# Four hybrid layers on one core: order, banks and buffers at the seams of the softmax layers

## The chip, the cores and the metric

The kernel runs on one core of a Trainium2 chip. What is measured is the time of one execution on the device, in microseconds (us); smaller is better.

## The reference

A sequence of 512 tokens with 1024 features passes four layers. Each layer has a mixer and a convolutional feed-forward part, each between two RMS norms with a residual:

```python
for layer in range(DEPTH):
    kind, j = layer % N_MIXERS, layer // N_MIXERS
    u = rms_norm(h, norm_g[layer, 0])
    u = nsa_mixer(...) if kind == 0 else stick_breaking_mixer(...) if kind == 1 else swa_sink_mixer(...)
    h = h + rms_norm(u, norm_g[layer, 1])
    u = conv_ffn(rms_norm(h, norm_g[layer, 2]), ...)
    h = h + rms_norm(u, norm_g[layer, 3])
```

The kinds are nsa, sb, swa, nsa. All have 16 heads of 64. The nsa mixer adds three gated attentions, over compressed, selected and window keys, with four key groups of four heads each; at this length selected and window keys see all earlier tokens, and each is a softmax over `q k^T / 8 - slope * distance` with the slope `2 ** (-(head + 1) / 2)`. The swa mixer is one softmax over the last 128 tokens with a sink term, with two key groups. The sb mixer weights values by sigmoids and a running product. The feed-forward part multiplies by 1024 x 5632, convolves over three tokens, gates with silu and multiplies by 2816 x 1024.

## The kernel before

Activations lie transposed: `h`, `xh`, `xl` are 8 chunks of 128 features by 512 tokens. Weight products are made from split numbers: a weight unit (128 x 1024) is loaded into a ring of four, ACT copies its high part (`split_hi`, L260), DVE subtracts the low part (`split_lo`, L266), and PE multiplies high by high, low by high and high by low (L304 to L306). Four units make a panel, which fills four of the eight PSUM banks; panel p takes banks 4 to 7 if p is odd. `panel_free` makes PE wait until the panel two before has been evacuated. Splits run three units ahead of PE.

Every engine has its own program, written out by hand in an order, with semaphores between them. Around a mixer it is this:

**Norm seam** (`pe_post`, `act_rn`, `dve_update`, `act_update`, `pool_h_squares`). PE sums squares, ACT makes the factor rn in two halves, DVE makes chunk 0 of the normed input (`dh`, L531, L534), and ACT copies it to `xh` (L577), for which the first products (`first_panel`, L332 to L338) wait. ACT splits a weight unit between rn and this copy. DVE then updates chunks 1, 2, 3, 0, 4 to 7 (L515, L516), each followed by the low part `xl` (L497) of the one before, and splits a unit (`split_lo`) after chunk 4. POOL adds the squares of h as soon as four are there. Chunks 0 to 3 come from a copy of the first output panel, chunks 4 to 7 from the second panel in PSUM. Only ahead of the sb layer (`stays(s)` false) the second panel is copied to `late_u` first, as the sb mixer's first panel goes to the same four banks.

**nsa mixer.** Query, compressed, gate, selected-key and window-key panels are multiplied in turn (`pe_nsa`); mixing of the compressed attention (`turned`, `mixed`, L1387 and L1395) is placed between the units of the window panel. Its third and fourth token blocks wait for the second of two `pt` buffers and for the output copies on ACT. Then `pe_attention` runs: four turns (`it`, one key group each), in which heads r, key kinds b (0 selected, 1 window) and four query tiles i follow each other. For each tile PE makes scores (L1052, L1053) four tiles ahead, DVE adds the distance table and takes the minimum (`biased`, L1121), ACT takes the exponential (L1213), PE turns the tile (L1063), ACT or DVE copies it to `pt`, PE multiplies by values (L1073), and DVE scales the output of a job (four tiles) into `om` (L1158), which POOL adds to `o` (L1267). Queries are split for each head by ACT and DVE into one of two `qs` buffers (L1205, L1104). POOL makes a table slope x distance for each head in one of two `tb` buffers (L1256). The window keys are copied (`act_k`) and their low parts made (`dve_k_low`) after the first four tiles of scores, ahead of everything else of the first turn. The score banks are 0 to 3, turned tiles and outputs are in 4 to 7.

**End.** When all jobs are added, `pe_out` turns `o` (L1291) column by column, ACT and DVE split it to `xh` and `xl`, four columns ahead of the first output product.

**swa mixer** (`pe_swa`). Queries, keys with values, and the second half of the queries are multiplied, DVE scales the queries (`dve_q`), then the same attention runs with b = 0 alone and 256 or 128 keys for a tile.

Of the kernel before, what the change touches and what calls it, by code (L numbers as in the profile page):

```python
# [6 lines left out]
F32 = mybir.dt.float32  # L7
# [12 lines left out]
H = 16  # L20
# [21 lines left out]
MIX_PANELS = {"nsa": 8, "sb": 7, "swa": 3}  # L42

MIX_READS = {"nsa": [(1, 0), (1, 0), (0, 1), (1, 0), (1, 1), (0, 0), (1, 1), (0, 0)], "sb": [(0, 0)] + [(1, 0)] * 4 + [(0, 1)] * 2,
# [59 lines left out]
def hybrid_layers(nc, ins, out, kinds=KIND):  # L104
# [7 lines left out]
    with ExitStack() as ctx:  # L112
# [53 lines left out]
        late_u = Space(40 * K, 48 * K)("late_u", [P, 4, T], F32)  # L166
# [10 lines left out]
        bank_done = sem("bank_done")  # L177
        units_done = sem("units_done")
# [113 lines left out]
        def unit_products(pe, p, u, xhi, xlo, first, last, i=None):  # L292


            pe.wait_ge(split_done, at(i, 4, u + 1))
            unit_matmuls(p, u, xhi, xlo, first, last, last)

        def unit_matmuls(p, u, xhi, xlo, first, last, by_bank):
# [4 lines left out]
            for k, o in order:  # L303
# [3 lines left out]
                if by_bank and k == 1 and o < 3:  # L307
                    mm.then_inc(bank_done, 1)
# [33 lines left out]
        def after_rsum(pe, p, u0, n, by_token):  # L342
# [9 lines left out]
            for j in range(4):  # L352
                pe.wait_ge(split_done, u0 + j + 1)
                unit_matmuls(p, u0 + j, lambda k: xh[:, 2 * j + k, :], lambda k: xl[:, 2 * j + k, :], j == 0, j == 3,
                             False) if j else first_by_bank(p, u0, sums_taken)
# [13 lines left out]
        def x_panel(pe, p, u0, n, i=None, step=0, turn=4, ready=None, output=False, before=None):  # L369

            panel_free(pe, p, i, step)
            for j in range(4):
                if before:
# [5 lines left out]
                             output and j == 3)  # L379
# [59 lines left out]
        def stays(s):  # L439


            return s % 2 == 0 or s + 1 == 2 * len(kinds) or kinds[(s + 1) // 2] != "sb"

        def dve_take_u(dve, s, p, u):
# [3 lines left out]
            dve.wait_ge(u_done, 4 * (s + 1) + 4 * sum(not stays(x) for x in range(s)))  # L448
            dve.sem_inc(evac_v, 1)

        def dve_sum_squares(dve, s, p):

            def take(o):
                if not stays(s):
                    dve.wait_ge(sq_done, 8 * s + 5 + o)
                    nc.vector.tensor_copy(late_u[:, o, :], bank(p, o)).then_inc(u_done, 1)

            dve.wait_ge(ss_done, s + 1)  # L460
            for o in range(3):
# [3 lines left out]
                if o < 2:  # L465
                    take(o)
            take(2)
            take(3)
            if not stays(s):
                dve.wait_ge(u_done, 4 * (s + 1) + 4 * sum(not stays(x) for x in range(s + 1)))  # L470
                dve.sem_inc(evac_v, 1)
# [19 lines left out]
        def dve_update(dve, ch, s, u, p, u_split, g_post, g_pre):  # L491
# [16 lines left out]
            def update(c):  # L508
                if c < 4:
                    src, d = u[:, c, :], dh[:, c % 2, :]  # L510
                elif stays(s):
                    src = d = bank(p, c - 4)
                else:
                    src, d = late_u[:, c - 4, :], dh[:, c % 2, :]
# [29 lines left out]
            low(2)  # L544
            update(0)
            for c in range(4, DC):
# [3 lines left out]
                if c == 4:  # L550
                    split_lo(dve, u_split)
            low(DC - 1)
            if stays(s):
                dve.sem_inc(evac_v, 1)

        def act_update(act, s, g_pre, first_units=False):
# [9 lines left out]
            if s < 0:  # L566
                for c in range(DC):
# [3 lines left out]
                    if first_units and c % 2:  # L571
                        split_hi(act, c // 2)
# [9 lines left out]
            for k, c in enumerate((1, 2, 3, 0, 4, 5, 6, 7)):  # L582
# [3 lines left out]
                square(k, c)  # L586

# [135 lines left out]
        def dve_ffn(dve, ch, l, n, s):  # L723
# [22 lines left out]
            dve_sum_squares(dve, s, plan.down_p[l] + 1)  # L746
# [19 lines left out]
        tb = soft("tb", [P, 2, T], F32)  # L766
# [38 lines left out]
        qs = Space(u2_at + 4 * K, u2_at + 8 * K)("qs", [P, 2, T], F32R)  # L805
        om = Space(u2_at, u2_at + 4 * K)("om", [P, 2, TC, DH], F32)
# [22 lines left out]
        v_passed = sem("v_passed")  # L829
        g_passed = sem("g_passed")  # L830
# [16 lines left out]
        k_ready = sem("k_ready")  # L847
        v_ready = sem("v_ready")
# [14 lines left out]
        tb_done = sem("tb_done")  # L863
# [14 lines left out]

        JOBS = {"nsa": 2 * H, "swa": H, "sb": 0, None: 0}
# [1246 lines left out]
```

## Time and profile before

| | us |
|---|---|
| median of 3 timed runs | 2695.88 (2695.68 to 2696.88) |
| profiled execution | 2692.94 |
| its span, first to last instruction | 2691.2 |
| PE busy | 2576.8 |
| DVE busy | 1652.7 |
| ACT busy | 1178.2 |
| POOL busy | 354.6 |

A busy time is the sum over an engine's instructions in that one execution; the chain that ended last lies on PE for 84% of the span and on DVE for 12%. In the rows, "idle <- releaser" is the time for which the engine stood still before an instruction, with what ended it.

### The profile page before, as it was taken

To read this page: it belongs to the slowest core of one execution; us is meant where nothing else is said; L and a number is where in the kernel's file an instruction comes from. 1 tells how busy PE (TensorE), PEld (TensorE's weight loads), DVE (VectorE), ACT (ScalarE), POOL (GpSimd) and SP (SyncE) were. 2 spreads that over 40 slices of the span, in tenths; PEclk is the share of its full clock that TensorE was granted. 3 is DMA by queue.
4 is the path that set the end of the run, shared out by engine and by line. 5 is a ranking of instruction groups with operands and counts; after the bars stand their busy time and mean duration, and the time that the engine had idled before them with its cause. 6 is when DMAs were issued, how large, how long until landed. Compare 5 with 4: busy or idle time off the path is not lost.

```text
span 2691.2 us, 38440 instructions
## 1 busy us (share of the span) xinstructions
PE 2576.8 (96%) x13432; PEld 2176.4 (81%) x13432; DVE 1652.7 (61%) x2869; ACT 1178.2 (44%) x1827; POOL 354.6 (13%) x298
## 2 busy tenths in 40 slices
PE   8989999999999889999999999999999899999997
PEld 6879978888878567888878878888779898788886
DVE  7567667665363857777355767764376675676733
ACT  4356544443232745444234544442333664444431
POOL 1012221110010002111010021110010121211100
PEclk9999999999999999999999999999999999999999
DMA  4400023322233012332322023323333000233321
GB/s 156 135 30 2 1 85 104 101 94 95 79 106 94 16 49 86 94 98 81 111 75 71 21 84 101 100 94 97 96 103 101 17 2 32 86 95 96 99 94 55
DMA packets 62054, 210.93 MB, mean 78 GB/s; under 512 B 8673, under 2 KB 10465, under 8 KB 61921
## 3 DMA queue, kind: packets, MB, share of 16 engines
q1 hardware_dynamic: 61920, 209.14, 24.6%
q8 instruction: 85, 1.39, 0.2%
q14 instruction: 49, 0.39, 0.0%
HBM read 207.02 MB, written 2.10 MB: 78 GB/s over the span
## 4 chain that ended last, share of the span: by engine, by line
PE 84%; DVE 12%; ACT 2%; issue 1%; DMA 0%; DVEq 0%; POOL 0%; SPq 0%; ACTq 0%; POOLq 0%
PE psum L304 20%; PE psum L305 20%; PE psum L306 20%; PE psum L1073 6%; PE psum L1063 3%; PE psum L917 2%; PE psum L918 2%; PE psum L919 2%; DVE left L1910 2%; PE psum L1053 2%; PE psum L1052 2%; PE psum L338 1%; DVE h L516 1%; DVE w_lo L266 1%; DVE xl L497 1%
## 5 line engine op out<-in xcount | busy, mean ns | idle before, releaser
L304 PE MATMUL psum<-xh,w_hi 128*128 128x512 f32 x1736 | 678.6, 391 | 4.6 <-DVEq L979 3.7
L305 PE MATMUL psum<-xh,w_lo 128*128 128x512 f32 x1736 | 677.3, 390 | 0.0
L306 PE MATMUL psum<-xl,w_hi 128*128 128x512 f32 x1736 | 676.9, 390 | 0.0
L266 DVE TENSOR_TENSOR w_lo<-w_raw,w_hi 128x1024 fp32r<-128x1024 f32 x226 | 288.7, 1291 | 520.5 <-ACT w_hi L260 518.8
L260 ACT ACTIVATE w_hi<-w_raw 128x1024 fp32r<-128x1024 f32 x226 | 235.5, 1057 | 572.9 <-PE psum L306 450.6
L304 PEld LDWEIGHTS psum<-xh,w_hi 128*128 128x128 f32 x1736 | 326.7, 188 | 73.5 <-DVEq L979 4.1
L306 PEld LDWEIGHTS psum<-xl,w_hi 128*128 128x128 f32 x1736 | 326.7, 188 | 67.6
L305 PEld LDWEIGHTS psum<-xh,w_lo 128*128 128x128 f32 x1736 | 326.7, 188 | 66.9
L720 DVE TENSOR_TENSOR w_lo<-w_raw,w_hi 128x1024 fp32r<-128x1024 f32 x160 | 209.2, 1308 | 253.6 <-ACT w_hi L716 253.6
L305 PE MATMUL psum<-ah,w_lo 128*128 (+1 forms) x704 | 274.2, 389 | 0.0
L304 PE MATMUL psum<-ah,w_hi 128*128 (+1 forms) x704 | 274.2, 389 | 0.0
L306 PE MATMUL psum<-al,w_hi 128*128 (+1 forms) x704 | 274.2, 389 | 0.0
L716 ACT ACTIVATE w_hi<-w_raw 128x1024 fp32r<-128x1024 f32 x160 | 168.4, 1052 | 234.8 <-PE psum L306 234.8
L691 POOL TENSOR_TENSOR cv<-cv 128x512 f32<-128x512 f32 x88 | 133.8, 1520 | 796.1 <-ACT cv L645 792.1
L1073 PE MATMUL psum<-v,pt 128*128 128x65 f32 x1504 | 212.1, 270 | 7.0 <-DVE pt L1169 5.4
L1073 PEld LDWEIGHTS psum<-v,pt 128*128 128x128 f32 x1504 | 204.3, 193 | 16.1 <-DVE pt L1169 9.7
L640 ACT ACTIVATE cv<-xo,conv_b,conv_w 128x512 f32<-128x512 f32 x176 | 129.2, 806 | 95.5 <-DVE xo L664 95.5
L673 DVE SCALAR_TENSOR_TENSOR cv<-xo,conv_w,cv 128x512 f32<-128x512 f32 x176 | 169.7, 1004 | 0.7 <-DVE xo L664 0.7
L1213 ACT ACTIVATE scores<-scores,mins 128x256 f32<-128x256 f32 (+1 forms) x320 | 162.0, 538 | 2.1 <-DVE mins L1121 1.5
L1121 DVE CUSTOM_DVE_ANT_0 scores<-psum,tb 128x512 f32<-128x512 f32 (+3 forms) x256 | 123.8, 485 | 57.0 <-PE psum L1053 53.7
L306 PEld LDWEIGHTS psum<-al,w_hi 128*128 128x128 f32 x704 | 132.2, 188 | 27.5
L304 PEld LDWEIGHTS psum<-ah,w_hi 128*128 128x128 f32 x704 | 132.2, 188 | 27.4
(193 smaller groups left out, 3870.9 us busy)
## 6 DMA issues: line engine op xcount, KB each, us to landing
w_raw<-w_up SPq DMA_DIRECT2D x176, 512.0 KB, 3.6
w_raw<-w_down SPq DMA_DIRECT2D x88, 512.0 KB, 3.6
w_raw<-nsa_in SPq DMA_DIRECT2D x56, 512.0 KB, 3.9
w_raw<-sb_in SPq DMA_DIRECT2D x24, 512.0 KB, 3.7
w_raw<-nsa_out SPq DMA_DIRECT2D x16, 512.0 KB, 3.6
w_raw<-swa_in SPq DMA_DIRECT2D x10, 512.0 KB, 3.7
w_raw<-sb_out SPq DMA_DIRECT2D x8, 512.0 KB, 3.6
w_raw<-swa_out SPq DMA_DIRECT2D x8, 512.0 KB, 3.7
```

Source lines behind the costliest of these rows:

```text
L260: nc.scalar.activation(w_hi[:, u % RING, :], w_raw[:, u % RING, :], ACT.Copy).then_inc(hi_done, 1)
L266: nc.vector.tensor_tensor(w_lo[:, u % RING, :], w_raw[:, u % RING, :], w_hi[:, u % RING, :].bitcast(F32), ALU.subtract).then_inc(split_don ...
L304: nc.tensor.matmul(bank(p, o), wh[:, k, o, :], xhi(k), start=(first and k == 0), stop=False)
L305: nc.tensor.matmul(bank(p, o), wl[:, k, o, :], xhi(k), start=False, stop=False)
L306: mm = nc.tensor.matmul(bank(p, o), wh[:, k, o, :], xlo(k), start=False, stop=(last and k == 1))
L640: nc.scalar.activation(cv[:, o, :], xo[:, o, 2:T + 2], ACT.Identity, bias=conv_b[:, bass.ds(cc, 1)], scale=conv_w[:, 2, bass.ds(cc, 1)]).t ...
L673: marks.append(ch.then(nc.vector.scalar_tensor_tensor(cv[:, o, :], xo[:, o, 1:T + 1], conv_w[:, 1, bass.ds(cc, 1)], cv[:, o, :], ALU.mult, ...
L691: nc.gpsimd.tensor_tensor(cv[:, 2 + a, :], cv[:, a, :], cv[:, 2 + a, :], ALU.mult).then_inc(prod_done, 1)
L716: nc.scalar.activation(w_hi[:, u % RING, :], w_raw[:, u % RING, :], ACT.Copy).then_inc(hi_done, 1)
L720: nc.vector.tensor_tensor(w_lo[:, u % RING, :], w_raw[:, u % RING, :], w_hi[:, u % RING, :].bitcast(F32), ALU.subtract).then_inc(split_don ...
L1073: mm = nc.tensor.matmul(psum[:, 6 + job % 2, i * (DH + 1):(i + 1) * (DH + 1)], pt[:, s % 2, j * P:(j + 1) * P], vt[b][:, k0 + j, it, :], s ...
L1213: nc.scalar.activation(sp_[:, s % 4, 0:nk * P], sp_[:, s % 4, 0:nk * P], ACT.Exp, scale=-1.0, bias=mins[:, c:c + 1]).then_inc(exp_done, 1)
```

## The change

- **Order of tiles.** In a turn all four heads run over the selected keys first (b = 0), then all four over the window keys. `qs` has four buffers; each head's queries are split in the turn before. The window keys' copies are cut up: POOL copies four halves ahead of its additions, ACT copies the four others (`win_twin`) and DVE makes the low parts (`win_low`) between tiles of the first turn.
- **No slope tables.** Queries are divided by the head's slope when split, and DVE's minimum multiplies by it; the distance table is the same for all heads, so POOL makes no tables and has nothing to do in the swa layer.
- **Banks.** `half_of(l, k)` is `k ^ 4`: scores are in banks 4 to 7, the rest in 0 to 3, in all mixers. The sb mixer has one panel number fewer, so its first panel goes to the other four banks; `late_u` and `stays` are gone.
- **Mixing.** The turning of blocks 2 and 3 stands in the middle of window unit 2, the mixing of 2 and 3 in the middle of unit 3; blocks 2 and 3 have `late_pt` buffers of their own. The first scores come before the wait for the evacuation of the window panel. ACT takes the last mixed outputs and the window values after two queries.
- **swa.** The first four tiles of scores stand ahead of the last unit of the second query panel, which tells of each bank (`qb_done`); DVE scales the queries bank by bank after its first four minima.
- **Turning of o.** Columns 0 to 2 are turned between the last tiles, and the first output unit starts with chunk 0 alone; its third and fourth banks wait for the last two jobs.
- **Norm seams.** ACT's weight split goes behind the first square of h, DVE's ahead of the update of chunk 0.

```diff
-MIX_PANELS = {"nsa": 8, "sb": 7, "swa": 3}
+MIX_PANELS = {"nsa": 8, "sb": 6, "swa": 3}
...
-            return [(b, r, i, win[i][0], win[i][1]) for r in range(R) for b in range(nb) for i in reversed(range(TC))]
+            return [(b, r, i, win[i][0], win[i][1]) for b in range(nb) for r in range(R) for i in reversed(range(TC))]
...
@@ dve_update
             update(3)
             low(2)
+            split_lo(dve, u_split)
             update(0)
             for c in range(4, DC):
                 dve.wait_ge(h_done, 8 * s + c)
                 update(c)
                 low(c - 1)
-                if c == 4:
-                    split_lo(dve, u_split)
@@ act_update
                 square(k, c)
+                if k == 0:
+                    split_hi(act, u_split)
@@ pe_attention, turn
                     if more or s + 4 < n:
                         scores(it, s + 4)
+                    elif kind == "nsa" and s + 1 < n:
+                        pe_turn_o(pe, l, s + 4 - n)
                     if s:
                         values(s - 1)
+                if kind == "swa":
+                    if not more:
+                        pe_turn_o(pe, l, 0)
+                        pe_turn_o(pe, l, 1)
                 values(n - 1)
+                if kind == "swa" and not more:
+                    pe_turn_o(pe, l, 2)
@@ dve_attention, biased
-                if i == TC - 1 and b == 0:
-                    dve.wait_ge(tb_done, it * R + (h0 + R * w + r + 1))
...
-                dve.sem_inc(v_passed, 1)
-                x = nc.vector.tensor_tensor_reduce(out=sp_[:, s % 4, 0:nk * P], in0=psum[:, s % 4, 0:nk * P], in1=bias,
-                                                   scale=1.0, scalar=lowest(it, w, r) if kind == "swa" else 3e38,
+                x = nc.vector.tensor_tensor_reduce(out=sp_[:, s % 4, 0:nk * P], in0=psum[:, half_of(l, s % 4), 0:nk * P], in1=away,
+                                                   scale=slope(R * (it + w) + r), scalar=lowest(it, w, r) if kind == "swa" else 3e38,
@@ dve_attention
+                    if kind == "nsa":
+                        if it == 0 and s in WIN_LOW:
+                            win_low(WIN_LOW.index(s))
+                        if more and s >= 16 and s % 4 == 3:
+                            queries(it + 1, s // 4 - R)
...
+        WIN_TWIN = (1, 6, 12, 17)
+        WIN_LOW = (2, 4, 8, 10, 14, 16, 20, 22)
@@ act_attention, ahead
                 queries(0, 0)
                 queries(0, 1)
+                if late and kind == "nsa":
+                    late()
+                    queries(0, 2)
+                    queries(0, 3)
@@ act_nsa
-            act_attention(act, l, "nsa", lambda: act_k(act, l, 1, 2, 2))
+
+            def between():
+                mixed(2)
+                mixed(3)
+                act_v(act, ch, 1, p0 + 6, u0 + 28)
+
+            act_attention(act, l, "nsa", between)
@@ pe_nsa
-            window(2)
+            window(2, turn_late)
             mixed(0)
-            turned(2)
-            turned(3)
-            window(3)
             mixed(1)
-            mixed(2)
-            mixed(3)
+            window(3, mix_late)
             pe.wait_ge(co_ready, TC * (k + 1))
-            panel_free(pe, W + 2)
...
+            def first(scores):
+                scores()
+                panel_free(pe, W + 2)
@@ pool_nsa
-            pool.wait_ge(cp_ready, 2 * (k + 1))
+            for g in range(G):
+                pool.wait_ge(kt_done, kc_before[l] + 2 + g // 2 + 1)
+                s_ = slice(64 * (g % 2), 64 * (g % 2) + 64)
+                nc.gpsimd.tensor_copy(kh[1][s_, g, :], ktmp[s_, g // 2, :]).then_inc(wkh_done, 1)
@@ pe_out
+            for k in range(2):
+                pe.wait_ge(o_ready, 8 * l + k + 1)
+                for o in range(4):
+                    if k == 0 and o >= 2:
+                        pe.wait_ge(om_done, jobs - 3 + o)
+                    mm = three(bank(p, o), wh[:, k, o, :], wl[:, k, o, :], xh[:, k, :], xl[:, k, :], k == 0, False)
+                if k == 0:
+                    pe_turn_o(pe, l, 3)
@@ pe_swa
+            def late_queries(first_scores):
+                def begin(j):
+                    if j == 3:
+                        panel_free(pe, p0 + 3)
...
+                        first_scores()
+
+                x_panel(pe, p0 + 2, u0 + 6, n, banks=qb_done, before=begin)
+                panel_free(pe, p0 + 4)
@@ dve_nsa
-            for c in range(2):
+            low_flat(0)
             dve_q(dve, ch, l, 0, p0 + 1, u0 + 8, -SCALE, qt)
+            low_flat(1)
```

## Rows read from the trace of the kernel before

**Rows 1.** Head of the page: busy time, share, instructions of each engine.
```profile
PE 2576.8 (96%) x13432; PEld 2176.4 (81%) x13432; DVE 1652.7 (61%) x2869; ACT 1178.2 (44%) x1827; POOL 354.6 (13%) x298
```

**Rows 2.** Busy time by stretches: us, engines (x instructions), granted clock, DMA share, GB/s.
```profile
143.40:181.44 38.04, 28.87 (x165) 25.36 (x165) 21.10 (x42) 18.16 (x32) 2.85 (x2) 0.87 0.13 42
...
181.40:217.30 35.90, 35.77 (x305) 34.84 (x305) 27.58 (x116) 24.65 (x53) 9.81 (x12) 1.00 0.01 1
...
1466.00:1522.00 56.00, 50.10 (x431) 47.34 (x430) 48.78 (x201) 42.85 (x117) 7.97 (x13) 1.00 0.00 1
```

**Rows 3.** Timeline of PE, first nsa attention start: start, us, operation, count, [idle<-releaser].
```profile
144.28 1.09 PE L1387 MATMUL psum<-ident,scores 128*128 128x128 f32 x8 [0.88 <-DVE scores L1614]
...
159.09 1.89 PE L1395 MATMUL psum<-cvb,pt 128*128 128x256 f32 x8
...
168.29 0.47 PE L1052 MATMUL psum<-kh,qs 128*128 128x512 f32 x1 [2.73 <-DVE qs L1104]
...
174.10 1.12 PE L1063 MATMUL psum<-ident,scores 128*128 128x128 f32 x4 [4.19 <-ACT scores L1213]
...
181.44 0.61 PE L1063 MATMUL psum<-ident,scores 128*128 128x128 f32 x4
```

**Rows 4.** Timeline of ACT in the same stretch.
```profile
159.29 1.57 ACT L995 ACTIVATE v<-psum,rt 128x256 f32<-128x256 f32 x4 [5.42 <-PE psum L919]
...
166.80 1.28 ACT L1205 ACTIVATE qs<-qt 64x512 fp32r<-64x512 f32 x2
...
168.10 5.20 ACT L953 ACTIVATE kh<-ktmp 64x512 fp32r<-64x512 f32 x8
...
173.33 1.23 ACT L1213 ACTIVATE scores<-scores,mins 128x512 f32<-128x512 f32 x2
```

**Rows 5.** DVE groups, shapes apart: shapes, count | busy us, mean ns | idle before.
```profile
L266 DVE TENSOR_TENSOR w_lo<-w_raw,w_hi 128x1024 fp32r<-128x1024 f32 x226 | 288.7, 1291 | 520.5 <-ACT w_hi L260 518.8 <-DVE qt L976 1.0 <-DVE xcf L1540 0.3
...
L1121 DVE CUSTOM_DVE_ANT_0 scores<-psum,tb 128x512 f32<-128x512 f32 x64 | 44.2, 691 | 46.2 <-PE psum L1053 46.2
...
L1104 DVE TENSOR_TENSOR qs<-qt,qs 64x512 fp32r<-64x512 f32 x48 | 32.9, 686 | 13.3 <-ACT qs L1205 11.9
```

**Rows 6.** Timeline of PE, end of the first nsa attention.
```profile
319.29 0.98 PE L1073 MATMUL psum<-v,pt 128*128 128x65 f32 x6
...
322.57 3.22 PE L1291 MATMUL psum<-ident,o 128*128 128x128 f32 x16 [2.29 <-POOL o L1267]
...
325.69 0.77 PE L304 MATMUL psum<-xh,w_hi 128*128 128x512 f32 x1
```

**Rows 7.** Timeline of PE, start of the swa attention.
```profile
1458.71 0.36 PE L1052 MATMUL psum<-kh,qs 128*128 128x256 f32 x1 [4.33 <-DVE qs L1104]
...
1460.50 0.69 PE L1063 MATMUL psum<-ident,scores 128*128 128x128 f32 x2 [0.66 <-ACT scores L1213]
...
1466.07 0.60 PE L1063 MATMUL psum<-ident,scores 128*128 128x128 f32 x2
```

**Rows 8.** Timeline of PE, end of the swa attention.
```profile
1525.88 0.47 PE L304 MATMUL psum<-xh,w_hi 128*128 128x512 f32 x1 [0.96 <-DVE xl L1302]
```

**Rows 9.** Timelines of ACT, DVE and PE in the norm seam after the first nsa.
```profile
374.48 0.42 DVE L534 TENSOR_TENSOR dh<-dh 128x256 f32<-128x256 f32 x1
...
374.63 1.04 ACT L260 ACTIVATE w_hi<-w_raw 128x1024 fp32r<-128x1024 f32 x1
...
375.58 0.71 ACT L577 ACTIVATE xh<-dh 128x256 fp32r<-128x256 f32 x2
...
386.14 2.31 DVE L266 TENSOR_TENSOR w_lo<-w_raw,w_hi 128x1024 fp32r<-128x1024 f32 x1
...
391.65 1.20 PE L338 MATMUL psum<-xl,w_hi 128*128 128x512 f32 x4 [0.82 <-DVE xl L497]
```

**Rows 10.** Timeline of PE in the norm seam before the sb layer.
```profile
755.89 1.20 PE L338 MATMUL psum<-xl,w_hi 128*128 128x512 f32 x4 [1.38 <-DVE xl L497]
...
761.20 1.21 PE L338 MATMUL psum<-xl,w_hi 128*128 128x512 f32 x4 [2.30 <-DVE xl L497]
```

More of the change, by code:

```diff
@@ L367, in first_by_bank, with x_panel @@
             mm.then_inc(units_done, 1)
-        def x_panel(pe, p, u0, n, i=None, step=0, turn=4, ready=None, output=False, before=None):
+        def x_panel(pe, p, u0, n, i=None, step=0, turn=4, ready=None, banks=None, before=None):
             panel_free(pe, p, i, step)
@@ L447, in dve_take_u, with dve_sum_squares @@
                 nc.vector.tensor_copy(u[:, o, :], bank(p, o)).then_inc(u_done, 1)
-            dve.wait_ge(u_done, 4 * (s + 1) + 4 * sum(not stays(x) for x in range(s)))
+            dve.wait_ge(u_done, 4 * (s + 1))
             dve.sem_inc(evac_v, 1)
[L451 to L458, printed above, removed]
+        def dve_sum_squares(dve, s):
             dve.wait_ge(ss_done, s + 1)
@@ L971, in dve_k_low, with dve_q @@
                 x.then_inc(k_ready, 1)
-        def dve_q(dve, ch, l, half, p, u_end, scale, dst):
-            dve.wait_ge(units_done, u_end)
+        def dve_q(dve, ch, l, half, p, u_end, scale, dst, banks=None):
+            if banks is None:
+                dve.wait_ge(units_done, u_end)
             for o in range(4):
+                if banks is not None and o < 3:
+                    dve.wait_ge(banks, 3 * sum(x == "swa" for x in kinds[:l]) + o + 1)
+                elif banks is not None:
+                    dve.wait_ge(units_done, u_end)
                 x = nc.vector.scalar_tensor_tensor(dst[:, 4 * half + o, :], bank(p, o), scale, rb[:], ALU.mult, ALU.mult)
@@ L1236, in ahead, with slope @@
                 queries(0, 1)
-            heads_loop(act, ahead, turn, late)
-            act.wait_ge(om_done, OM_FREE + jobs_before[l + 1])
+                if late and kind == "nsa":
+                    late()
+                    queries(0, 2)
+                    queries(0, 3)
+            heads_loop(act, ahead, turn, late if kind == "swa" else None)
+        def slope(head):
+            return float(np.float32(2.0 ** (-8.0 * (head + 1) / H)))
         def esink_bias(it, r):
             return sinks[:, bass.ds(it * R + r, 1)]
+        WIN_TWIN = (1, 6, 12, 17)
+        WIN_LOW = (2, 4, 8, 10, 14, 16, 20, 22)
         def pool_attention(pool, l, kind):
@@ L1277, in ahead @@
[L1277 to L1294 removed]
+                for job in range(2 * R):
+                    add(job)
```

352 lines of the change are left out of this document (183 added, 169 removed).

## The prediction

> **What bounds the kernel now.** I read the head of the page first: TensorE (PE) is busy for 2576.8 us, 96% of the span [rows 1]. No other engine is near that, so the change can win only time in which PE stands still, or in which it runs at half clock. The second view is the busy time by stretches. Inside an nsa attention there is nothing to win: one of its four turns takes 35.90 us with PE busy for 35.77, which is 4.49 us for each of eight jobs (a job is four tiles of one head). In the swa attention PE is busy for 50.10 of 56 us and DVE for 48.78; but the stretch in which the first nsa attention starts has PE busy for 28.87 of 38.04 us, with a mean granted clock of 0.87 [rows 2]. The third view is therefore the timeline at each seam: what PE waits for, and how long its matmuls stay stretched afterwards.
>
> The profiled execution took 2692.94 us (span 2691.2), the median of the timed runs is 2695.88. I make the sum on the profiled one and take the difference off the median.
>
> **1. Start of the nsa attention, two layers.** Before, 38.04 us lie between the end of window unit 1 (144.28 less a wait of 0.88 = 143.40) and the first transposes of job 1 (181.44). PE's waits there are 0.88 for DVE's weighting, 2.73 for the split queries and 4.19 for the first exponentials [rows 3]. ACT causes the large ones: it copies queries only after the last mixed output, and then 5.20 us of window keys before its first exp [rows 4]. Job 0 takes 181.44 - 174.10 = 7.34 us against 4.49, its matmuls being at the lower level, 1.2 GHz instead of 2.4.
> After, tiles of selected keys come first, so the window keys' copies and subtractions leave this spot. PE's work to the end of the window panel is the 14.81 us from 144.28 to 159.09 plus three mixing groups of 1.73 each (their 1.89 less the tail under the next) [rows 3]: 20.0. Two of these groups and two of the turning groups now stand in the middle of a unit, which covers their waits. Then come four tiles of scores, 174.10 - 4.19 - 168.29 = 1.6, written to banks that the window panel does not use. What is late next is ACT: from the panel's end it runs v, 1.57, two query halves, 1.28 together, and the first exp, half of 1.23 [rows 4]: 3.5 us, of which 1.6 lie beside the scores. With 0.2 for semaphores PE waits 2.1. Job 0 is 4.5 at full clock. Sum 20.0 + 1.6 + 2.1 + 4.5 = 28.2 us against 38.04. A gap of that size does slow PE a little: after the 2.29 at the end of this attention sixteen transposes take 3.1 us to the next start [rows 6], where eight took at most 1.09 before [rows 3]. I put this at 0 to 1.7 us, the upper end a good half of the 2.85 that job 0 loses now. So 8.1 to 9.8 is won; I take 8.6, twice: **17.2**. If ACT stays late as before it is 4 each.
> The window keys' low parts, four subtractions of 0.69, like those of the queries of the same shape [rows 5], and four copies, at most as long, 5.5 us in all, now lie on DVE between tiles in the first six jobs of turn 0. DVE is busy there for 27.58 x 6/8 = 20.7 of 27 us [rows 2], so they just fit, but for jobs that also carry queries. I charge 0.5 for each layer, bounds 0 and 3: **-1.0**.
>
> Of POOL, first the row. While it adds squares in a norm seam, the split of weights, with two SBUF inputs, takes 2.31 us [rows 9]; its mean over the run is 1.29 [rows 5]. The Trainium skill's page "SBUF — State Buffer" (the section on ports) says that a GpSimd operation and a DVE operation with two SBUF inputs shut each other out for a whole instruction; the trace agrees in direction. By that rule POOL's four new key copies would meet the query subtractions at the start, and the sum would be some 2 us smaller; by the rows it is unchanged, as POOL's tables, removed now, left the query subtractions at a mean of 0.69 [rows 5].
>
> **2. End of the nsa attention, two layers.** Before: last values until 320.27, a wait of 2.29 for POOL's last addition, sixteen transposes from 322.57, first output product at 325.69 [rows 6]. After: twelve of the transposes stand between the last tiles (at the 8 in 1.09 of rows 3 at most 1.6 us, so PE ends at about 321.7 with them done), their ACT and DVE halves run beside the last tiles, and the first products need column 0 alone. Products of the fourth bank wait for the last head's output, which comes within the old 2.3 us (that held the addition too) and is covered by nine products. First product at 321.8, the fourth column still to turn, 0.5: 325.69 - 321.8 - 0.5 = 3.4, and up to 0.4 from the slow stretch. I take 3.6, twice: **7.2** (bounds 4 and 8).
>
> **3. Start of the swa attention.** Before, the query panel ends at 1458.71 - 4.33 = 1454.38, and job 1 begins at 1466.07 [rows 7]: 11.7 us. After: the scores (1460.50 - 0.66 - 1458.71 = 1.1) come before the last unit, whose products (5 to 6 us, as a window unit) hide minima, exponentials and three banks of queries; only the fourth bank is open, 0.7 like a 512-wide operation in rows 5, with 0.15 for its semaphore. A job is 56/15 = 3.7 us here. 1.1 + 0.85 + 3.7 = 5.7. Won: **6.0** (bounds 4 and 6.5). Queued behind DVE's waits for the banks are the next minima; four tiles are scored by then, which is PE's cover.
>
> **4. End of the swa attention.** Before, the first output product is at 1525.88 after a wait of 0.96 for xl [rows 8], with four columns turned. After, two columns are turned ahead of the last values and one behind; I put the first product at about 1523.3 and the fourth column at 0.5: **2.1** (bounds 1 and 2.6).
>
> **5. Six norm seams.** ACT's weight split, 1.04, stands ahead of the first xh although dh is there at 374.48 + 0.42 = 374.90; xh starts at 375.58. It moves behind, and PE's first product is 0.7 earlier. DVE's split moves ahead of the update of chunk 0, when POOL has not started: 1.3 instead of 2.31. PE's stall at chunk 4 is 0.82 and ends with an xl of DVE [rows 9]; that xl comes about 1.1 earlier, and 0.8 to 1.1 can be gained, less if the next chunk then waits. 0.8 each: **4.8**. Bounds -2 (the split, earlier in the chain, delays chunk 3) and 7.
>
> **6. Seam before the sb layer.** late_u vanishes: updates from it read two SBUF operands beside POOL's additions, and PE waits 1.38 and 2.30 [rows 10], 3.68 against the 0.82 of the other seams. With the gain of part 5: **3.6** (bounds 2 and 4.5).
>
> **Edits at nothing.** The slopes folded into queries and minima leave number and shape of DVE's operations; a minimum with a scale could cost more or, without its marker and the table's wait, less. No row separates them: bounds -3 and +3 us over 80 jobs, I take 0. In the nsa start the flat low part and the queries change places; the weight split that PE's next unit needs still ends behind both, so the evacuation wait is only replaced: 0. Banks exchanged by four keep their distances: 0. One table fewer on SP's queue: 0.
>
> Sum: 17.2 - 1.0 + 7.2 + 6.0 + 2.1 + 4.8 + 3.6 = 39.9 us. From 2692.9 that is 2653.0; from the median, 2656.0.
>
> **Rivals.**
> *ACT's queue takes the place of the wait.* If v, queries, exps and the window twins line up on ACT, the gap at the nsa start stays at 5 us with a long slow stretch behind it: part 1 gives 8 instead of 17.2; and if DVE's earlier split delays chunk 3, part 5 gives 0. 39.9 - 9.2 - 4.8 = 25.9: 2670. For it: ACT releases the 4.19 wait now. Against: 5.20 us of its queue is gone.
> *The slow stretches go too.* They follow stalls [rows 3, 6]. If shorter stalls are followed by none, 1.2 more at each nsa start, up to 1.3 at each of seven norm seams and some tenths elsewhere come on top, 12 us in all: 2644. For it: the stalls shrink everywhere. Against: the gap ahead of each norm seam's first product hardly does. The Trainium skill's page "TensorE: Matmul & The Clock Gate" (Part 1) adds that the point at which the gate acts varies between runs; by it such a gain is not to be counted on.
> *Slower: the scaled minimum makes DVE the bound.* A job has four, and there are 64 nsa and 16 swa jobs. DVE's slack in an nsa job is (35.9 - 27.6)/8 = 1.0 us, in a swa job (56 - 48.8)/15 = 0.5 [rows 2]. Only where each minimum (now 0.69 at 512 wide [rows 5]) is over 0.4 us longer, so that 64 x 0.6 and 16 x 1.1 are lost, is the gain of 40 used up; at 0.45 it is 64 x 0.8 + 16 x 1.3 = 72 and the time 2728. Nothing in the operands speaks for it: one PSUM and one SBUF input, as before.
> *It does not do what it says:* the new waits (window keys, POOL's additions, the fourth bank) hold PE as long as the old ones, and time stays within 5 us of 2696.
>
> **How the numbers follow.** Forecast 0.62 (2648 to 2664), ACT's queue 0.18 (2664 to 2680), no slow stretches 0.14 (2640 to 2648), slower 0.03, nothing 0.03. The range that leaves out 2 in 10 is 2642 to 2670. About 0.2%, 5.4 us, is what a measurement of this kernel can tell from no change: faster 0.95, same 0.02, slower 0.03.
>
> **What would show it.** In the profile after: PE waits about 2 us at the first transposes of the nsa attention, and nowhere for qs; no wait for POOL where o is turned; at the swa start about 1 us instead of 4.33; xl stalls gone or under 0.5, and none of 2.30 before sb; the split in the update at 1.3. The prediction is wrong where the first nsa turn takes over 37 us, where a 128x512 minimum is longer than 0.69, or where waits for the window keys or for POOL's additions appear.

## The result and the profile after

The changed kernel takes 2666.53 us (median of 4 runs, 2662.36 to 2667.27) against 2695.78 for the kernel before (2695.33 to 2696.88): ratio 0.9887, 95% interval 0.9871 to 0.9903. The forecast was 2656.0 us, its range 2642 to 2670. The profiled execution took 2667.27 us with a span of 2665.3, so 25.9 us are gained between the two spans, where the sum said 39.9.

The head of the page, which answers to [rows 1]: PE is busy for 7 us less, so over two thirds of the gain is time in which PE stood still.

```profile
PE 2569.6 (96%) x13432; PEld 2165.7 (81%) x13432; DVE 1645.6 (62%) x2865; ACT 1178.4 (44%) x1819; POOL 310.4 (12%) x258
```

Busy time by stretches, as in [rows 2]: the start of the first nsa attention from window unit 1 to job 1, its first turn, its second turn, and 54 us of the swa attention.

```profile
145.00:174.60 29.60, 26.86 (x167) 24.53 (x165) 18.33 (x38) 15.29 (x27) 2.43 (x4) 0.94 0.12 41
174.60:209.90 35.30, 35.30 (x303) 34.41 (x302) 31.75 (x123) 27.41 (x55) 5.85 (x8) 1.00 0.01 1
209.90:245.27 35.37, 35.37 (x306) 34.62 (x305) 28.73 (x117) 25.45 (x53) 5.86 (x8) 1.00 0.01 2
1446.00:1500.00 54.00, 50.19 (x437) 47.54 (x436) 48.47 (x201) 42.21 (x117) 0.00 (x0) 1.00 0.01 2
```

Timeline of PE at the starts and ends of the attentions, which answers to [rows 3, 6 to 8]: the first transposes of the first nsa attention, the start of job 1, its last values, the first output product, the first transposes and the start of job 1 of the swa attention, and its first output product.

```profile
169.04 1.09 PE L1056 MATMUL psum<-ident,scores 128*128 128x128 f32 x4 [2.74 <-ACT scores L1236]
...
174.60 0.61 PE L1056 MATMUL psum<-ident,scores 128*128 128x128 f32 x4
...
311.60 0.98 PE L1066 MATMUL psum<-v,pt 128*128 128x65 f32 x6
313.16 0.47 PE L902 MATMUL psum<-xh,w_hi 128*128 128x512 f32 x1 [0.58 <-DVE xl L1333]
...
1441.96 0.44 PE L1056 MATMUL psum<-ident,scores 128*128 128x128 f32 x2 [0.84 <-DVEq L971]
...
1445.35 0.39 PE L1056 MATMUL psum<-ident,scores 128*128 128x128 f32 x2
...
1500.72 0.47 PE L902 MATMUL psum<-xh,w_hi 128*128 128x512 f32 x1 [0.46 <-DVE xl L1333]
```

The waits of 4.19, 2.73, 2.29 and 4.33 us are gone; 2.74, 0.58 and 0.84 stand in their place. The seams gave what was forecast, or more. The missing gain must have been lost elsewhere, and it is found in the same timeline a little later, in the output projections of the first nsa layer and of the swa layer:

```profile
324.65 1.03 PE L1323 MATMUL psum<-ident,o 128*128 128x128 f32 x8
...
327.26 0.50 PE L304 MATMUL psum<-xh,w_hi 128*128 128x512 f32 x1 [1.57 <-DVE xl L1333]
...
332.88 1.03 PE L1323 MATMUL psum<-ident,o 128*128 128x128 f32 x8
336.94 0.47 PE L304 MATMUL psum<-xh,w_hi 128*128 128x512 f32 x1 [3.03 <-DVE w_lo L266]
...
1524.43 0.77 PE L304 MATMUL psum<-xh,w_hi 128*128 128x512 f32 x1 [3.03 <-DVE w_lo L266]
```

Two new waits, 1.57 and 3.03 us, stand behind the turning of columns 4 and 5 and of 6 and 7, in each of three layers. The timelines of ACT and DVE show what is queued at the second:

```profile
333.51 1.09 ACT L1329 ACTIVATE xh<-psum 128x512 fp32r<-128x512 f32 x2 [7.14 <-PE psum L1323]
334.14 1.29 DVE L1333 TENSOR_TENSOR xl<-psum,xh 128x512 fp32r<-128x512 f32 x2 [6.94 <-ACT xh L1329]
...
334.48 3.90 ACT L260 ACTIVATE w_hi<-w_raw 128x1024 fp32r<-128x1024 f32 x4
```

ACT stands still for 7.14 us, until PE turns column 6. Only then come columns 6 and 7, and behind them the splits of four units of weights, the first of which PE needs at once. In the kernel before, PE turned these columns one unit earlier, with a unit's products (5.5 us) between the turning and the need.

### The profile page after: what moved, and what is told of

The parts are those of the page before. It is cut to its first block, busy times and chain, and to the rows that moved or that the text cites. A ratio compares the mean times of both kernels' runs of the same rounds, so it can differ in the third digit from the quotient of the medians.

```text
span 2665.3 us, 38269 instructions
## 1 busy us (share of the span) xinstructions
PE 2569.6 (96%) x13432; PEld 2165.7 (81%) x13432; DVE 1645.6 (62%) x2865; ACT 1178.4 (44%) x1819; POOL 310.4 (12%) x258
## 4 chain that ended last, share of the span: by engine, by line
PE 86%; DVE 11%; ACT 1%; issue 1%; DMA 0%; DVEq 0%; SPq 0%; ACTq 0%
PE psum L304 20%; PE psum L305 20%; PE psum L306 20%; PE psum L1066 6%; PE psum L1056 3%; PE psum L902 2%; PE psum L904 2%; PE psum L903 2%; DVE left L1986 2%; PE psum L1046 2%; PE psum L1045 2%; DVE xl L477 2%; DVE h L494 1%; PE psum L338 1%; DVE share L1992 1%
## 5 line engine op out<-in xcount | busy, mean ns | idle before, releaser
L304 PE MATMUL psum<-xh,w_hi 128*128 128x512 f32 x1712 | 671.1, 392 | 18.2 <-DVE w_lo L266 13.5
L305 PE MATMUL psum<-xh,w_lo 128*128 128x512 f32 x1712 | 669.5, 391 | 0.0
L306 PE MATMUL psum<-xl,w_hi 128*128 128x512 f32 x1712 | 669.1, 391 | 0.0
L266 DVE TENSOR_TENSOR w_lo<-w_raw,w_hi 128x1024 fp32r<-128x1024 f32 x226 | 279.0, 1250 | 516.4 <-ACT w_hi L260 515.1
L698 DVE TENSOR_TENSOR w_lo<-w_raw,w_hi 128x1024 fp32r<-128x1024 f32 x160 | 209.3, 1308 | 253.6 <-ACT w_hi L694 253.6
L305 PEld LDWEIGHTS psum<-ah,w_lo 128*128 128x128 f32 x704 | 132.2, 188 | 27.3
```

The lines of the kernel that those rows point to most:

```text
L266: nc.vector.tensor_tensor(w_lo[:, u % RING, :], w_raw[:, u % RING, :], w_hi[:, u % RING, :].bitcast(F32), ALU.subtract).then_inc(split_don ...
L304: nc.tensor.matmul(bank(p, o), wh[:, k, o, :], xhi(k), start=(first and k == 0), stop=False)
L305: nc.tensor.matmul(bank(p, o), wl[:, k, o, :], xhi(k), start=False, stop=False)
L306: mm = nc.tensor.matmul(bank(p, o), wh[:, k, o, :], xlo(k), start=False, stop=(last and k == 1))
L698: nc.vector.tensor_tensor(w_lo[:, u % RING, :], w_raw[:, u % RING, :], w_hi[:, u % RING, :].bitcast(F32), ALU.subtract).then_inc(split_don ...
```

## The experiments

**1. The turning alone.** In the changed kernel each pair of columns is turned one unit earlier:

```diff
-                if j >= 2:
-                    pe_turn_o(pe, l, 2 * j)
-                    pe_turn_o(pe, l, 2 * j + 1)
+                if j <= 2:
+                    pe_turn_o(pe, l, 2 * j + 2)
+                    pe_turn_o(pe, l, 2 * j + 3)
```

> The changed kernel, with TensorE's turning of columns 4 and 5 put back ahead of the second unit of the output projection, and of 6 and 7 ahead of the third, as before the change. Theory (the turning, moved one unit later, is what cost the missing gain): the two waits in each softmax layer, 1.57 us for a low part and 3.03 us for the split of the weights, both go, 3 x 4.6 = 13.8 us, and up to 3.4 us of half-clock stretches behind them: 2649 to 2653 us. Rival (the projection waits because ACT's and DVE's queues are full there, wherever TensorE turns): the waits only move to the units before, and the time stays at 2660 us or above.

Measured: 2646.9 us (ratio to before 0.9813, interval 0.9797 to 0.983), 19.6 less than the changed kernel. Both waits are gone in all three layers, and the time is lower than the theory said. PE's timeline of the swa layer shows the sum of squares that ends the projection, first in the changed kernel and then in this one; the first products stood at 1500.72 and 1497.03:

```profile
1554.77 0.67 PE L410 MATMUL psum<-ss,ones 128*128 128x256 f32 x2
```

```profile
1543.27 0.67 PE L410 MATMUL psum<-ss,ones 128*128 128x256 f32 x2
```

So the projection took 54.05 us and takes 46.24. In the three layers it was 51.38, 54.05 and 54.13 with the late turning, against 46.23, 46.24 and 46.21: 20.9 us. Of these 13.8 are the waits; most of the rest is half clock, in two of the layers. The theory holds; its bound on the stretches, 3.4, was too small.

**2. The same edit in the kernel before.** `turn_next` there turns columns `2 * j` and `2 * j + 1` for `j in (2, 3)`, not `2 * j + 2` and `2 * j + 3` for `j in (1, 2)`.

> The kernel before, with one edit: in the output projection TensorE turns columns 4 and 5 ahead of the third unit and 6 and 7 ahead of the fourth, as in the changed kernel, not one unit earlier. Theory (the place of the turning alone makes the two waits): waits of about 1.6 and 3.0 us appear in each of three softmax layers, 13.8 us, and up to 10 us of half-clock stretches behind them: 2709 to 2720 us. Rival (the waits come from the first unit's new form, whose fourth column is turned late and shifts the queues of ACT and VectorE): no such waits, 2695 to 2699 us.

Measured: 2717.75 us against 2695.88 (ratio 1.0087, interval 1.007 to 1.0104), 21.9 slower. The waits appear without anything else of the change:

```profile
340.38 0.50 PE L304 MATMUL psum<-xh,w_hi 128*128 128x512 f32 x1 [1.57 <-DVE xl L1302]
...
350.06 0.47 PE L304 MATMUL psum<-xh,w_hi 128*128 128x512 f32 x1 [3.04 <-DVE w_lo L266]
```

The three projections take 52.90, 52.37 and 53.13 us against 46.11, 45.73 and 46.21, 20.4 more. With experiment 1 this closes the question: the edit costs about 20 us in either kernel, and needs nothing else of the change for it.

**3. The queue beside the late turning.** Turning stays late; ACT and DVE split the next unit of weights ahead of columns 6 and 7:

```diff
             for c in range(DC):
+                if c == 6:
+                    split_hi(act, plan.out_u[l] + AHEAD)
```

> The changed kernel, with the late turning of columns 4 to 7 kept, but on ACT and DVE the split of the next unit of weights now stands ahead of columns 6 and 7. Theory (TensorE turns too late, so that both the split and the columns come late): the 3.03 us wait shrinks to about the 1.57 us of the other one, 3 x 1.5 = 4.4 us, 2660 to 2663 us. Rival (the split's place in the two queues alone is the cause): the 3.03 us go altogether, 9 us or more, at or under 2658 us.

Measured: 2656.25 us (0.9851, 0.9834 to 0.9867), 10.3 less than the changed kernel. The number is the rival's (at or under 2658), but the trace shows the theory's mechanism: the wait did not vanish, it became one of 1.57 us for xl, like the other (six in the run, 9.4 us). That is 4.4 us; with it the half clock behind the 3.03 went, and the three projections take 49.93, 49.99 and 49.94 us, 9.7 less together. A time alone would have decided this one wrongly.

**4. DVE's split in the norm seams, alone in the kernel before.**

```diff
             low(2)
+            split_lo(dve, u_split)
             update(0)
...
-                if c == 4:
-                    split_lo(dve, u_split)
```

> The kernel before, with one edit of the change: in the norm seams DVE splits its unit of weights ahead of the update of chunk 0, not behind that of chunk 4; ACT's split stays where it was. Theory (DVE's split beside GpSimd's additions causes the stall of 0.82 us at chunk 4): each of six seams is 0.4 to 0.8 us shorter and the time 2691 to 2693.5 us. Rival 1 (the earlier split, longer in the chain than what it saves, delays chunk 3): the seams are as long or up to 0.4 us longer, 2695 to 2698 us. Rival 2 (the whole gain of the seams, 0.65 us each, comes from ACT's split): no difference, 2695.8 us.

Measured: 2688.77 us against 2696.53 (ratio 0.997, interval 0.9959 to 0.998), 7.8 less, more than the theory. Rows of DVE and PE in its first seam; the L411 and L386 rows are the sums of squares that begin and end it:

```profile
374.50 0.67 PE L411 MATMUL psum<-ss,ones 128*128 128x256 f32 x2
...
384.79 1.22 DVE L266 TENSOR_TENSOR w_lo<-w_raw,w_hi 128x1024 fp32r<-128x1024 f32 x1
...
402.90 1.02 PE L386 MATMUL psum<-ss,ones 128*128 128x512 f32 x2
```

The split takes 1.22 instead of 2.31 us [rows 9], and the seam 28.40 instead of 29.07 (371.80 to 400.87). Five seams are 0.63 to 0.68 shorter, the one after the sb mixer 2.2. Only the seam ahead of the sb layer stays long, 31.35 us against 31.40: it still has `late_u`. In the changed kernel that one takes 28.40 too, so `late_u` cost 3.0; no run takes it out by itself, but the other edits there gain nothing (this experiment and the next). The seven seams add up to 5.6 us; where the other 2.2 of the 7.8 come from is open.

**5. ACT's split put back,** in the changed kernel, ahead of the first xh.

> The changed kernel, with ACT's split of weights put back ahead of the norm seams' first xh, DVE's split left ahead of the update of chunk 0. Theory (the seam's length is set by DVE's chain of updates and low parts, in which ACT's split has no part): the first product of a seam comes 0.6 us later, and the seam from the first sum of squares to the next sum is as long as before, 28.4 us: within 1 us of the changed kernel, 2665 to 2668 us. Rival (half of each seam's gain is ACT's): each of seven seams is 0.6 us longer, and the time is 2670 to 2671 us.

Measured: 2667.17 us (0.9889, 0.9872 to 0.9905). PE's rows of the first seam:

```profile
364.30 0.67 PE L410 MATMUL psum<-ss,ones 128*128 128x256 f32 x2 [0.15 <-DVE ss L451]
...
368.73 0.36 PE L332 MATMUL psum<-xh,w_hi 128*128 128x256 f32 x1 [2.47 <-ACT xh L554]
...
392.73 1.02 PE L385 MATMUL psum<-ss,ones 128*128 128x512 f32 x2
```

The first product waits 2.47 us instead of 1.85, and the seam takes 28.43 us, against 28.34 (364.54 to 392.88) in the changed kernel. ACT's part of the edit gains nothing: with it PE starts 0.6 earlier and loses as much again further on in the seam, while DVE's chain is the same. With experiment 4 this says that the gain of six seams is that of DVE's split, and that of the seventh is `late_u`'s.

**6. The markers.** From the kernel before, the increments of `v_passed` and `g_passed` are taken out:

```diff
-                dve.sem_inc(v_passed, 1)
                 x = nc.vector.tensor_tensor_reduce(out=sp_[:, s % 4, 0:nk * P], in0=psum[:, s % 4, 0:nk * P], in1=bias,
```

> The kernel before, without the two markers that VectorE and GpSimd set between the tables of slopes and their readers (the readers' own semaphores still order them). It asks what made a job of the nsa attention 4.41 us instead of 4.49 in the changed kernel. Theory (the markers' extra instructions delay VectorE's minimum and with it TensorE): four turns of the first nsa attention take 35.3 us each instead of 35.9, 64 x 0.08 = 5 us, 2691 us. Rival (the new order of jobs or the query tile of four buffers does it): the turns stay at 35.9 us and the time at 2696 us.

Measured: 2689.55 us against 2696.34 (ratio 0.9973, interval 0.9962 to 0.9985), 6.8 less. (The profiled execution is the longest of its seven, 2693.12 us; the stretches below are read from it.) One turn (eight jobs) of the second nsa attention, from one start to the start eight jobs later, in the kernel before, without markers, and in the changed kernel:

```profile
2125.62 0.61 PE L1063 MATMUL psum<-ident,scores 128*128 128x128 f32 x4
...
2161.63 0.60 PE L1063 MATMUL psum<-ident,scores 128*128 128x128 f32 x4
```

```profile
2125.36 0.61 PE L1063 MATMUL psum<-ident,scores 128*128 128x128 f32 x4
...
2160.98 0.60 PE L1063 MATMUL psum<-ident,scores 128*128 128x128 f32 x4
```

```profile
2124.87 0.61 PE L1056 MATMUL psum<-ident,scores 128*128 128x128 f32 x4
...
2160.23 0.61 PE L1056 MATMUL psum<-ident,scores 128*128 128x128 f32 x4
```

A turn takes 36.01, 35.62 and 35.36 us: the markers explain 0.39 of the 0.65. The theory had said 35.3 us for a turn, so it holds in part. The other 0.26 is open; the order of jobs, the four query buffers and the missing slope tables were not tried apart. From its first transposes to the wait for the last output the swa attention takes 58.10 us without markers (1459.98 to 1518.08), against 61.52 before (1460.50 to 1522.02). Job 0 gives 1.1 of these 3.4 us, with a shorter stretch at half clock; the jobs behind it run at full clock but for the first and give 2.3.

**7 to 10. What is left in the changed kernel.** These add to the early turning of experiment 1. The kernel called "the run before the last" in the first expectation is that of experiment 1.

```diff
+                    queries(0, 2)
+                    queries(0, 3)
                     late()
-                    queries(0, 2)
-                    queries(0, 3)
```

> The kernel of the run before the last (early turning of columns 4 to 7), and beside it, at the start of the nsa attention, the second pair of query halves is made before the window values and the window keys, so that ACT has less in its queue ahead of the first exponentials. Theory (ACT's queue sets the gap of 2.74 us there): the gap shrinks to about 1.5 us, 1.3 us in each of two layers, 2646 to 2650 us. Rival (the first exponentials wait for the minima of DVE or for TensorE's scores): the gap stays within 0.3 us and the time at that of the early turning alone.

Measured: 2641.13 us (0.9792, 0.9776 to 0.9809), 5.8 less than experiment 1, yet the gap only shrank from 2.74 to 2.39. Rows of ACT, DVE and PE:

```profile
165.50 1.29 DVE L982 TENSOR_TENSOR ktmp<-psum,rb 128x512 f32<-128x512 f32 x2
...
167.72 1.23 ACT L1235 ACTIVATE scores<-scores,mins 128x512 f32<-128x512 f32 x2 [1.14 <-DVE mins L1117]
...
168.59 1.09 PE L1056 MATMUL psum<-ident,scores 128*128 128x128 f32 x4 [2.39 <-ACT scores L1235]
```

On the gap itself the rival is nearly right (it allowed 0.3): ACT now waits for a minimum, which waits on DVE behind the evacuation of the window keys. The two gaps give 0.7 us. The time is neither the theory's nor the rival's: in the first nsa layer job 0, behind the gap, took 8.03 us in experiment 1 and 5.69 here, which is clock (mean granted clock 0.74 and 0.91 from 164 to 184 us); in the second layer it took 5.75 and 5.86. I do not put the other 5 us down to the edit. Next, `biased(0, 0)` goes ahead of `late()` on DVE:

> The kernel with the early turning of columns 4 to 7 and the second pair of query halves ahead of the window values, and beside it VectorE makes the minimum of the first tile before it evacuates the window keys (1.29 us). The gap at the first transposes of the nsa attention was 2.39 us there, with ACT idle for 1.14 us ahead of the first exponential, for a minimum. Theory (the evacuation in VectorE's queue sets the gap): the first exponential starts behind the window values, 1.1 us earlier, and the gap is 1.3 us, so 2 x 1.1 less, 2637 to 2640 us. Rival (the transposes wait for the evacuation of the window panel itself, whose banks they write): the gap shrinks by no more than 0.5 us, 2640 to 2643 us.

Measured: 2642.07 us (0.9795, 0.9778 to 0.9811). The gap is 1.44 us in both layers, as the theory said, and no half clock follows it (mean granted clock 1.00 from 164 to 184 and from 2060 to 2080 us, where the run before had 0.91 in both). The time of the runs doesn't show it: the spans are 2640.9 and 2643.7, the medians 2642.07 and 2641.13. Stretches at half clock that stand elsewhere in one run and not in the other are as large as the gain.

```profile
167.34 0.63 PE L1056 MATMUL psum<-ident,scores 128*128 128x128 f32 x4 [1.44 <-ACT scores L1236]
```

Third, on the kernel without that edit, the split that PE waits for goes ahead of the second flat low part:

```diff
             low_flat(0)
+            split_lo(dve, u0 + 6 + AHEAD)
             dve_q(dve, ch, l, 0, p0 + 1, u0 + 8, -SCALE, qt)
+            split_lo(dve, u0 + 7 + AHEAD)
             low_flat(1)
```

> The kernel with the early turning and the second pair of query halves ahead of the window values, and beside it, in the mixing panels of the nsa layers, VectorE splits the unit of weights that TensorE waits for (2.23 us at 68.7 us) before the second flat low part (2.23 us long), behind the queries. Theory (the low part in the queue is the whole wait): TensorE waits for the queries' banks or the split alone, under 0.3 us, and the half-clock stretch of 3.4 us behind it goes too: 2 x (2.0 + 1.7) = 7 us less, 2634 to 2637 us. Rival (the low part, later, now holds the flat products): as much is lost a unit later, 2640 to 2642 us.

Measured: 2638.08 us (0.9782, 0.9766 to 0.9799). PE's wait was 2.23 us in the changed kernel (first row) and 1.80 before the change; here (second row) the product starts 1.8 us earlier and the wait is under 0.3:

```profile
68.73 0.47 PE L304 MATMUL psum<-xh,w_hi 128*128 128x512 f32 x1 [2.23 <-DVE w_lo L266]
```

```profile
66.89 0.47 PE L304 MATMUL psum<-xh,w_hi 128*128 128x512 f32 x1
```

On the wait and the clock behind it the theory is right: from 68 to 75 us the mean granted clock is 1.00, with the wait it was 0.76. But the time fell by 3.1 us and not by 7, which is neither the theory's number nor the rival's; new stretches at half clock stand at 1530 to 1560 us (0.94) and 2240 to 2280 us (0.96), where the run before had 1.00.

All four edits together:

> The changed kernel with four edits: early turning of columns 4 to 7, the second pair of query halves ahead of the window values, the first minimum ahead of the window keys' evacuation, and the weight split ahead of the second flat low part. Theory (the gains at separate places add up): 1.0 us less in each of two nsa starts than with the other three, 2635 to 2637 us. Rival (what a shorter wait saves there comes back as half-clock time elsewhere): 2638 us, as with the other three.

Measured: 2634.82 us (2634.34 to 2635.52; ratio 0.9776, interval 0.9759 to 0.9792), 61 less than before and 31.7 less than the changed kernel. That is a little under the theory's range. The gap is 1.44 us in both layers, again with no half clock behind it, and the time is 3.3 us under that of the third variant, of which the two gaps are 1.9; in the second variant the same edit showed nothing. So the shorter waits are all there in the trace, but how much of each reaches the time is blurred by stretches at half clock that come and go elsewhere.

## Why the prediction was right, and where it failed

The time lies in the range, 10.5 us above the likeliest value, in the band that the prediction had given to ACT's queue (2664 to 2680, chance 0.18), and for a reason that is in none of the cases. That it lies in the range is luck: a loss of 21.5 us was left out, and the terms that were counted gave 8.7 us more than forecast. Term by term, measured between the marks that the prediction used:

| part | predicted us | measured us |
|---|---|---|
| nsa starts, two, window low parts included | 16.2 | 8.4 + 9.7 |
| nsa attentions from job 1 to the first output product, two | 7.2 | 5.7 + 5.4 |
| swa start | 6.0 | 6.4 |
| swa attention from job 1 to the first output product | 2.1 | 4.4 |
| seven norm seams | 8.4 | 8.6 |
| output projections, from first product to norm seam | 0 | -21.5 |

The lines add up to 27.1. From the start to window unit 1 the first layer is 1.6 us longer than before, the same stretch of the second layer 0.1, and small stretches give back 0.5: that makes the 25.9 of the spans. Of the 1.6 most is half clock behind the wait at the flat low part; the stretch before (first row) and after:

```profile
68.00:75.00 7.00, 6.46 (x31) 5.20 (x32) 4.51 (x5) 1.52 (x5) 0.00 (x0) 1.00 0.56 170
68.00:75.00 7.00, 6.27 (x21) 5.00 (x22) 4.58 (x5) 0.96 (x1) 0.00 (x0) 0.76 0.65 233
```

Parts 1 to 4 have no run of their own; their amounts are read between marks of the two traces. Only the norm seams, the markers and the turning were taken apart by runs.

**The step that failed** is in parts 2 and 4. They end at the first output product, with the fourth column's 0.5 us on the path, and take what follows as unchanged. But `pe_out` was rewritten, and with it columns 4 and 5 went from ahead of unit 1 to ahead of unit 2, and 6 and 7 from unit 2 to unit 3. The queues behind a moved step, which the prediction follows at the starts of the attentions, were not followed for these four columns: ACT's and DVE's halves of the columns are 0.6 and 0.69 us each, in series with PE, and ACT's and DVE's splits for the following units stand behind them. That was readable in the code and its diff, with the durations at hand in the trace. It cost about 20 us in experiments 1 and 2; without it the change would have gained 49.6, more than the sum.

**Part 1 was right**, in place and in size: 28.2 us were forecast from window unit 1 to job 1, and 29.60 and 28.40 measured. PE waits 2.74 us (2.1 forecast), and nowhere for qs. v (1.56) and queries (1.28) stand one behind the other ahead of the first exponential, as worked out. In the first layer job 0 is slow for a while (mean clock 0.94 over the stretch), in the second it is not: the 0 to 1.7 us charged for it were both seen. The window keys' low parts cost nothing: the first turn takes 35.30 us with DVE busy for 31.75, so the 1.0 charged was too much. What was said of POOL's key copies and the query subtractions, that they leave each other unchanged, was not put to the test: the copies lie at 165.87 to 168.48 us, and the subtractions at 157.88 and 168.37. Later in the turns the new order does bring the two engines together, and there the subtraction isn't unchanged (last section).

**Parts 2, 3 and 4.** The waits for POOL and for qs are gone. The swa start came out at 0.84 us of wait against 0.85 forecast. Part 4 gave 4.4 us, beyond its bound of 2.6; the 2.3 us of the markers (experiment 6) account for the difference from the 2.1 forecast.

**Parts 5 and 6** were right in the sum and wrong in a mechanism. 4.8 + 3.6 were forecast. Five seams gave 0.65 to 0.73, the one ahead of the sb layer 3.0, and the one after the sb mixer 2.25, because in the execution before its stall at chunk 4 was 2.33 us and not the 0.82 of [rows 9]. The stalls for xl aren't gone or under 0.5, as the signs had it: in four of the seven seams one of 0.93 us stands one chunk earlier, and these seams are no longer than the others (28.38 to 28.40 us). The split is 1.1 us shorter, but in the first seam one more xl now lies beside POOL's additions and takes 1.82 us where it took 0.74, and two of the later chunks come 3.1 us apart that came at most 2.9 apart: part of the gain is lost again. ACT's half of the edit, counted as 0.7 us of earlier start, gives nothing (experiment 5): a later link of the chain, DVE's updates and xl, sets the seam's length.

**Edits at nothing.** The minimum with a scale is as long as before (0.69 us at 128x512), so the slower rival is out. Its limit was miscounted, too: 64 x 0.6 and 16 x 1.1 are 56 us, so a gain of 40 would be used up by minima 0.35 longer, not 0.4. But zero was wrong for the markers, which the text named: 0.39 us per turn is 3.1 us in the eight turns of the two nsa layers, if all are like the one measured, and the swa attention gained 2.3 behind its job 0 (experiment 6). They are the larger part of what parts 2 and 4 gained beyond the sum. The flat low part, also at nothing, cost something in both nsa layers: I had said that the wait was only replaced, which is so, but by a longer one (2.23 us for 1.80, 2.16 for 1.85), and in the first layer half clock followed it.

**The rivals.** The time of 2670 for ACT's queue at the nsa start came near, with another cause. A queue behind late work was the cause, but at the other end of the attention.

## What to carry to other kernels

Follow a moved step to the end of the routine that was rewritten, not to the first instruction that comes earlier: here the edit that hid a seam took away the cover of the next two. A unit's products between the turning and its use were worth 20 us over three layers, while the seams around them were being shortened by tenths. And where two engines feed a chain, an earlier start on the one that isn't last gains nothing; its effect is read from the length of the whole seam, not from the first wait.

## What the runs showed of the hardware

**Equal stalls, unequal clocks.** The wait of 3.03 us is the same in all three layers of the changed kernel. Busy time by stretches behind it, the first nsa layer and then the swa layer; the number after POOL is the granted clock:

```profile
337.00:341.00 4.00, 4.00 (x18) 3.32 (x19) 3.20 (x3) 1.38 (x2) 0.00 (x0) 1.00 0.77 215
1522.00:1526.00 4.00, 1.56 (x4) 1.30 (x5) 3.86 (x5) 3.87 (x5) 0.00 (x0) 0.68 0.20 36
1526.00:1530.00 4.00, 4.00 (x11) 3.13 (x10) 1.70 (x2) 0.00 (x0) 0.00 (x0) 0.50 0.89 304
1530.00:1534.00 4.00, 4.00 (x18) 3.28 (x18) 0.00 (x0) 1.04 (x1) 0.00 (x0) 0.96 0.47 184
```

In the first, PE went on at 2.4 GHz; in the second it ran at 1.2 GHz for some 7 us, and the projection took 54.05 instead of 51.38 us. So the same stall cost 2.7 us more in one layer than in another. The Trainium skill's page "TensorE: Matmul & The Clock Gate" (Part 1) says that the point of transition varies with the phase in which the work falls; the rows agree in that equal stalls were answered differently.

**Two SBUF inputs beside POOL.** The split takes 1.22 us ahead of POOL's additions and 2.31 beside them, in the same seam, with nothing else changed (experiment 4). The changed kernel shows it a second time. Its query subtraction (L1103, both inputs in SBUF) takes 1.12 us in the first three turns of each nsa attention, where an addition of POOL (L1300) has started 0.15 us earlier, and 0.69 in the swa attention, where POOL does nothing. The mean over the run is 0.90, against the 0.69 of [rows 5]. From the timelines of DVE and POOL:

```profile
228.38 1.12 DVE L1103 SCALAR_TENSOR_TENSOR qs<-qt,qs 64x512 fp32r<-64x512 f32 x1
228.23 0.73 POOL L1300 TENSOR_TENSOR o<-o,om 128x256 f32<-128x256 f32 x1 [3.67 <-DVE om L1154]
...
1443.65 0.69 DVE L1103 SCALAR_TENSOR_TENSOR qs<-qt,qs 64x512 fp32r<-64x512 f32 x1
```

DVE has room for it there: the second turn takes 35.37 us. In the norm seams an operation with one input in PSUM (L515) keeps its 0.75 to 0.76 us beside the same additions. The Trainium skill's page "SBUF — State Buffer" (the section "Who interferes with whom") has such an operation and GpSimd's shut each other out; the direction agrees, and whether the 1.1 and 0.43 us are waiting or slower work no row tells.

**A marker is not free.** An instruction that only increments a semaphore has no busy time in the profile. Yet those ahead of each of DVE's minima and of POOL's operations, taken out together, made a job of the nsa attention 0.05 us shorter (0.39 for eight), in turns in which PE is busy for 35.77 of 35.90 us [rows 2].
